# When ScalarE may start the first hidden step of the next expert: after its own in blocks, or after the two out blocks behind them

## The reference

```python
combine = jnp.sum(one_hot(top_idx, 8) * gates[..., None], axis=-2)   # top 2 of 8
out = jnp.zeros_like(h)
for e in range(8):
    g, u = jnp.split(h @ w_in[e], 2, axis=-1)       # w_in[e]:  1024 x 7168
    out = out + combine[..., e:e + 1] * ((silu(g) * u) @ w_out[e])   # w_out[e]: 3584 x 1024
```

## Time and profile before

| what | value |
|---|---|
| median of three executions | 1921.71 us (1921.23 to 1921.82) |
| the profiled execution: its time | 1919.38 us |
| its span, first to last instruction | 1917.6 us |
| TensorE busy | 1787.8 us (93% of the span) |
| VectorE busy, ScalarE busy | 478.5 us (25%), 392.6 us (20%) |
| the experts, first in block to last out block | about 914 to 1893 us of the span |
| mean granted TensorE clock | 0.964 of full speed |

### The profile page before, as it was taken

How to read it: one execution, slowest core, us unless ns; L and a number is a source line. 1 busy time by engine, 2 the same in 40 slices (tenths; PEclk the granted TensorE clock), 3 DMA queues, 4 the chain that set the end, 5 groups by cost and what they waited for, 6 DMA issues and landing times.

```text
span 1917.6 us, 36307 instructions
## 1 busy us (share of the span) xinstructions
PE 1787.8 (93%) x16358; PEld 1057.6 (55%) x16358; DVE 478.5 (25%) x826; ACT 392.6 (20%) x694; POOL 34.9 (2%) x71
## 2 busy tenths in 40 slices
PE   5999879999999799876999999999999999999995
PEld 2755678888888588446345353453533534445342
DVE  3326362232333752655000101101000010010103
ACT  3236242221322521662000100001010010100001
POOL 1000100000000000010000000000000000000000
PEclk9999889999999899986999999999999999999997
DMA  9357713223242131575899999999999999999970
GB/s 371 111 177 250 242 48 105 94 90 108 88 132 98 51 134 64 182 285 229 308 361 364 336 364 369 364 366 334 380 364 351 368 343 376 364 349 363 357 295 24
DMA packets 141162, 477.46 MB, mean 249 GB/s; under 512 B 11168, under 2 KB 35096, under 8 KB 122576
## 3 DMA queue, kind: packets, MB, share of 16 engines
q1 hardware_dynamic: 137344, 467.64, 66.7%
q0 software_dynamic: 3664, 7.48, 1.1%
HBM read 473.96 MB, written 1.13 MB: 248 GB/s over the span
## 4 chain that ended last, share of the span: by engine, by line
PE 49%; DVE 1%; ACT 0%; issue 0%; DVEq 0%; ACTq 0%
PE ps L966 48%; PE ps L1397 1%; DVE residual L1912 0%; ACT silu_g L909 0%; PE ps L1393 0%; DVE y_split L1890 0%; PE ps L1455 0%; DVE work L1978 0%; DVE residual L1980 0%; DVE work L1974 0%; DVE residual L1913 0%; ACT y_split L924 0%; ACT silu_g L910 0%; DVEq L1958 0%; DVE y_acc L1903 0%
## 5 line engine op out<-in xcount | busy, mean ns | idle before, releaser
L966 PE MATMUL ps<-w_hi,h_t 128*128 128x512 f32 (+1 forms) x960 | 298.0, 391 | 19.0 <-DVE h_t L1555 7.2
L966 PE MATMUL ps<-w_moe,h_te 128*32 128x256 f32 (+1 forms) x3520 | 298.3, 495 | 16.4 <-DVE residual L1913 16.4
L966 PE MATMUL ps<-h_t,w_hi 128*128 128x512 f32 (+1 forms) x768 | 222.6, 375 | 5.4 <-DVE h_t L1555 5.4
L966 PEld LDWEIGHTS ps<-w_moe,h_te 128*32 128x32 f32 x3520 | 113.6, 111 | 194.5 <-issue 140.3
L966 PE MATMUL ps<-w_raw,h_te 128*32 128x256 f32 (+2 forms) x3648 | 216.8, 396 | 0.0
L1502 DVE TENSOR_TENSOR w_lo<-w_raw,w_hi 128x2048 fp32r<-128x2048 f32 x58 | 132.9, 2292 | 330.6 <-ACT w_hi L626 330.2
L966 PEld LDWEIGHTS ps<-w_hi,h_t 128*128 128x128 f32 x960 | 182.9, 193 | 58.7 <-issue 8.2
L966 PE MATMUL ps<-w_lo,h_t 128*128 128x512 f32 (+1 forms) x480 | 187.3, 390 | 0.0
L1912 DVE TENSOR_TENSOR residual<-silu_g,ps 128x512 f32<-128x512 f32 (+1 forms) x32 | 19.8, 618 | 648.7 <-ACT silu_g L910 648.7
L626 ACT ACTIVATE w_hi<-w_raw 128x2048 fp32r<-128x2048 f32 x58 | 110.8, 1914 | 325.3 <-PE ps L966 316.4
L966 PEld LDWEIGHTS ps<-w_raw,h_te 128*32 128x32 f32 x3648 | 113.0, 110 | 100.2 <-issue 61.3
(11 more groups left out here) (231 smaller groups left out, 1211.7 us busy)
## 6 DMA issues: line engine op xcount, KB each, us to landing
w_moe<-in_expert_in_w_dram SPq DMA_DIRECT2D x110, 1024.0 KB, 6.3
w_raw<-in_expert_out_w_dram SPq DMA_DIRECT2D x62, 1024.0 KB, 7.3
w_raw<-in_expert_in_w_dram SPq DMA_DIRECT2D x50, 1024.0 KB, 7.6
w_raw<-in_ada_w_dram SPq DMA_DIRECT2D x48, 1024.0 KB, 5.0
w_moe<-in_expert_out_w_dram SPq DMA_DIRECT2D x34, 1024.0 KB, 6.9
work<-in_expert_in_w_dram SPq DMA_DIRECT2D x32, 1024.0 KB, 7.3
w_raw<-in_expert_in_w_dram SPq DMA_DIRECT2D x64, 512.0 KB, 5.0
w_raw<-in_ffn_in_w_dram SPq DMA_DIRECT2D x44, 512.0 KB, 4.9
```

The costliest lines, as they stand in the source:

```text
L966: return pe.matmul(out_, l, r, start=first, stop=last, skip_group_check=True)
```

## The change

`silu` takes a third argument, `ahead`, the number of out blocks that lie between the in blocks of its step 0 and the count 8. At the boundary it is called with `len(step_blocks("out", STEPS - 1))`, which is 2, so it waits for a count of `used` that is lower by two: the count after in block 7 of step 0, ahead of the two out blocks. The call for expert 0 (`silu(0, 0)`), which has no out blocks behind its in blocks, keeps the count. All instructions, and their order on each engine, stay as they are; the values of seven waits on ScalarE change.

```diff
             def step_end(s_):
-                return 8 + max(n for n, x in enumerate(LAST) if x[:2] == ("in", s_)) + 1 if s_ else 8
-
-            def silu(e, s_):
+                return 8 + max(n for n, x in enumerate(LAST) if x[:2] == ("in", s_)) + 1
+
+            def silu(e, s_, ahead=0):
                 J = STEPS * NE * rnd + e * STEPS
                 h, q = WIDTH[s_] // 2, WIDTH[s_] // 4
-                act.wait_ge(used, base + e * EB + step_end(s_))
+                if s_:
+                    act.wait_ge(used, base + e * EB + step_end(s_))
+                else:
+                    act.wait_ge(used, base + e * EB + 8 - ahead)
                 act.wait_ge(act_done, FG + J + s_)
...
                 transposed(e, 3)
                 if not last:
-                    silu(e + 1, 0)
+                    silu(e + 1, 0, len(step_blocks("out", STEPS - 1)))
                 yhi(e, last)
```

## The result

The changed kernel takes 1898.09 us (median of four executions, 1896.74 to 1900.37) against 1921.47 us before (four executions, 1918.33 to 1921.82). The ratio is 0.9889, with a 95% interval of 0.9876 to 0.9902: 1.1% faster, 23 us. In a second set of executions, taken with the last experiment, the medians are 1898.69 and 1921.42 us, 22.7 us apart. The forecast was 1899.2 us in a range of 1895.5 to 1904.5. The profiled execution has a span of 1895.3 us, where before had 1917.6 and the forecast 1895.1.

What follows compares the result with a forecast made beforehand. The prediction took TensorE to bound the experts, with stalls at seven boundaries: 15.7 us of stall plus 6.8 us of low clock make 22.5 us, so 1921.71 − 22.5 = 1899.2 us, range 1895.5 to 1904.5.

Steps and rivals of the forecast that it cites:

- The bound: Among the experts: TensorE, busy 93% of the span, is the bound and not the loads.
- The stall: At seven expert boundaries TensorE idles 2.0 us for silu and product; each costs 2.24 us, together 15.7 us, which go.
- The clock: Behind four of seven boundaries TensorE's low clock costs 1.70 us more each, 6.8 us together; all four go.
- the case that they stay: Rival at the boundaries: the stall goes, the low clock stays in part or whole; 1906.0 us with all; chance 0.10.
- behind every second stall: At the expert boundaries: the low clock follows stalls in turn, low and full, four low and three full.
- The sum: Whole kernel: 15.7 + 6.8 = 22.5 us less, from 1921.71 to 1899.2 us, a span of about 1895.1.
- The cover: At the boundary: two out blocks, 5.2 us, hide the 2.0 us chain from silu to TensorE's release; 3.2 us left.
- the copy behind it: Behind boundary silu: ScalarE's result copy and VectorE's remainder bring no new wait; remainder done at about 5.9, 8 us cover.
- The loads: Expert weight loads must reach 368 GB/s against 358; with 25 us of spare time they cost nothing.
- Rival B: Among the experts: loads take over, spare time is used up, TensorE waits for weights; about 1921 us; chance 0.03.
- C: Over the experts: the chip cuts TensorE's clock under some 930 us of load without pauses; 1926 us; chance 0.02.
- D: At the boundary: silu is held by something other than `used`, so the change does nothing; 1921.7 us; chance 0.01.

Runs made afterwards that it cites:

- the last experiment: Changed kernel with ScalarE's copy of an expert's result reported in two parts, bank 3 and bank 4: 1896.06 us beside the changed kernel's 1898.69 us.
- four silus: Changed kernel with each boundary silu done four times over, same result: 1898.0 us, ratio to before 0.9884.
- the kernel with three stalls: Changed kernel with the old silu wait put back at three of the seven boundaries: 1907.12 us, ratio to before 0.9931.
- the one with seven silus: Changed kernel with each boundary silu done seven times over: 1920.2 us, ratio to before 1.0005.
- the ten-block kernel: Changed kernel with each load of the experts issued ten blocks later: 1909.49 us, ratio to before 0.9947.
- nine silus: Changed kernel with each boundary silu done nine times over: 1945.14 us, executed once.

## Why the prediction was right

**The bound.** TensorE bounded the experts, and each stall at a boundary was worth its full length. With the stalls gone TensorE is busy 934.00 of 934.00 us, by the window above.

**The stall.** Seven times 2.24 us, as the sum had it: the waits went from eight to one. The experiments put it back in four lengths (1.4, 2.0, 2.3 and 4.1 us), and the time followed.

**The clock.** That all four low stretches would go was a choice, with 0.10 for the case that they stay. They went, in both profiles of the changed kernel and with four silus. The reason that I gave (they stand behind stalls only) holds; "behind every second stall" was what one profiled execution of before showed, and the kernel with three stalls and the one with seven silus don't have it. That there were four, and so the 6.8 us, is known for that execution alone: the timed ones have no trace, and later executions of before took 1917.1 to 1922.0 us. That the number came out within 1.1 us has some luck in it.

**The sum.** From the release behind expert 0's stall to the end of the last out block it was 936.47 to 1893.11 us before, and is 935.80 to about 1870.8 now: 956.6 against 935.0, 21.6 us less, where the sum had 22.5. The other 0.7 us of the span's 22.3 were gained ahead of the experts, which the change doesn't touch. The missing 0.9 us can be placed: the piece of the chain that holds step 3's in blocks and the gather varies in the changed kernel. Over experts 0 to 6 it sums to 0.9 us more than seven times its usual 24.74. Here it is at expert 2, at its usual length, and at expert 6, 0.4 us longer:

```profile
1239.33 24.74 PE ps L969 x416
...
1718.71 25.15 PE ps L969 x406
```

**The cover, the copy behind it.** Both held: 3.2 us of cover, and a chain of 2.0 us that even one block hides. VectorE's remainder is done 5.9 us after the boundary (1061.94, by its timeline), as forecast, and nothing waits for it until the last expert.

**The loads.** They went from 359 GB/s (over the two experts from the first to the third boundary) to 369 without a wait of TensorE. The spare time was still enough with eight blocks of it taken away. Rival B is dead as it was put (a mean rate that can't be kept); the ten-block kernel shows a different cost of the loads, landings longer than the time that the ring leaves them. The figure of 358 GB/s for a core's transfers from HBM, from the Trainium skill ("DMA: Bandwidth & Descriptors", section "Where 436 GB/s comes from"), is no limit here: three experts in a row have 369 GB/s, 360 us long. That section gets the figure by sharing a stack's rate between two cores, and this kernel runs on one; no run here has a second core loading beside it.

**The other rivals.** C (a lower clock under a load without pauses) did not occur: 1.00 over 934 us. D fell with the first profile.

## What to carry to other kernels

A wait on a counter can name a later event than the one whose data it needs; compare each wait's value with what the waiting instruction reads, above all where a loop's last step is set up differently from the others. Work that lies in the order behind a producer hides its consumer only when the consumer is released ahead of it. A short stall of TensorE can cost more than its length, since a low clock may follow; the price of a stall is the time from one finished block to the next, with and without it, at several places. A buffer ring's spare time is counted against the slowest landing: here 12.9 us from issue to use were enough and 7.7 us were not, with landings of up to 8.9 us.

## What the runs showed of the hardware

At the boundaries, the low clock came behind none of seven stalls of 1.4 us, five of ten of 2.0 us (two kernels), two of seven of 2.3 us, and seven of seven of 4.1 us. Between 2.0 and 2.3 us the length didn't decide it, and expert 0's stall of 2.0 us never brought it in thirteen profiled executions. Each length but 2.0 us is one execution. A stall of 2.0 us that got the low clock cost 1.70 us on top of its 2.24.

TensorE's start among the experts differs by up to 3 us between profiled executions of kernels that don't differ up to there: TensorE comes back from expert 0's stall at 935.80 us in the changed kernel and at 938.79 us with nine silus. This scatter is as large as the 2.3 us between the profiled and the timed executions of before. Where in the first 930 us it arises was not looked into.

The in blocks of step 3, the part of an expert with the most matmuls for its length, took up to 0.8 us more in some executions, at zero to four of the experts; of this the profile names at most 0.3 us, as "issue", which is no wait for another engine. What holds them up stays open.
